# Second norm of a two-layer trunk kernel: row sums inside the output projection, scaling by rows in the lookup, first query weights loaded early

## The reference, cut to what matters

```python
for l in range(2):
    # mixing part: norm, one wide projection, four kinds of heads (4 of each)
    branches = ...                                   # retention, hgrn, gated delta, attention
    h = x + sum(gates * merged, axis=2) @ w_out      # output projection, 1024 x 1024
    y = h + peer_ffn(rms_norm(h, norm_ffn), peer_wq, peer_keys, peer_u, peer_v)

def peer_ffn(x, wq, keys, u_tab, v_tab):
    q = (x @ wq).reshape(blk, 8, 2, 128)             # 16 query tiles of 128 columns
    s = einsum('nhpd,hpkd->nhpk', q, keys)           # then two rounds of top 16, softmax g
    act = gelu(einsum('nhkd,nd->nhk', u_tab[idx], x))
    return einsum('nhk,nhkd->nd', g * act, v_tab[idx])
```

## Time and profile before

| what | value |
|---|---|
| median of 3 runs | 6624.28 us (6622.97 to 6627.76) |
| profiled execution, its own time | 6626.84 us |
| its span | 6625.2 us |
| TensorE busy | 6229.8 us, 94% of the span |
| VectorE, ScalarE busy | 54%, 32% |
| mean granted TensorE clock | 0.964 of 2.4 GHz |
| DMA | 804 MB, 121 GB/s over the span |

### The profile page before, as it was taken

How to read it: one execution, slowest core, us unless ns; L and a number is a source line. 1 busy time by engine, 2 the same in 40 slices (tenths; PEclk the granted TensorE clock), 3 DMA queues, 4 the chain that set the end, 5 groups by cost and what they waited for, 6 DMA issues and landing times. The chain is left out here.

```text
span 6625.2 us, 109110 instructions
## 1 busy us (share of the span) xinstructions
PE 6229.8 (94%) x42728; PEld 5837.3 (88%) x42728; DVE 3589.1 (54%) x6665; ACT 2142.5 (32%) x3178; POOL 0.7 (0%) x6
## 2 busy tenths in 40 slices
PE   8999988979999999999989999889799999999999
PEld 6777768979999989999967777689799999899999
DVE  3444353337788875555434443433377888755554
ACT  2333333222234442222223333232222344422222
POOL 0000000000000000000000000000000000000000
PEclk9999988989999999999999999899899999999999
DMA  3212212224346665454322122122243466654543
GB/s 103 66 50 76 65 40 74 81 89 122 113 131 181 181 196 213 168 181 167 134 94 70 50 73 70 37 75 77 92 124 112 128 188 179 194 210 170 180 167 138
DMA packets 494713, 804.32 MB, mean 121 GB/s; under 512 B 81716, under 2 KB 303156, under 8 KB 476212
## 3 DMA queue, kind: packets, MB, share of 16 engines
q1 hardware_dynamic: 494436, 800.67, 37.9%
HBM read 616.20 MB, written 186.72 MB: 121 GB/s over the span
## 5 line engine op out<-in xcount | busy, mean ns | idle before, releaser
L1652 PE MATMUL ps<-parts,wh 128*128 128x288 f32 x9216 | 1856.2, 297 | 43.7 <-DVE wl L1882 43.7
L1652 PEld LDWEIGHTS ps<-parts,wh 128*128 128x128 f32 x9216 | 1472.9, 188 | 46.9 <-DVE wl L1882 44.6
L1652 PE MATMUL ps<-parts,wl 128*128 128x288 f32 x4608 | 1356.5, 294 | 0.0
L2091 PE MATMUL ps<-parts,vh 128*128 128x320 f32 (+1 forms) x4096 | 886.5, 297 | 37.5 <-DVE gl L2163 32.1
L2091 PE MATMUL ps<-gl,vh 128*128 128x320 f32 (+1 forms) x4096 | 878.7, 295 | 0.0
L2091 PE MATMUL ps<-parts,vl 128*128 128x320 f32 (+1 forms) x4096 | 874.5, 294 | 0.0
L1652 PEld LDWEIGHTS ps<-parts,wl 128*128 128x128 f32 x4608 | 867.8, 188 | 0.0
L2168 DVE TENSOR_TENSOR vl<-third,vh 128x512 fp32r<-128x512 f32 x512 | 352.7, 689 | 675.5 <-ACT vh L2111 675.5
L2111 ACT CAST vh<-third 128x512 fp32r<-128x512 f32 x512 | 317.1, 620 | 1163.4 <-PE ps L2091 1132.2
L2091 PEld LDWEIGHTS ps<-parts,vh 128*128 128x128 f32 x4096 | 623.7, 188 | 50.0 <-issue 32.7
L2091 PEld LDWEIGHTS ps<-parts,vl 128*128 128x128 f32 x4096 | 631.4, 189 | 0.0
(11 more groups left out here) (384 smaller groups left out, 8159.1 us busy)
## 6 DMA issues: line engine op xcount, KB each, us to landing
raw<-in_u SPq DMA_DIRECT2D x256, 512.0 KB, 4.0
third<-in_v SPq DMA_DIRECT2D x512, 256.0 KB, 2.8
activated<-go SPq DMA_DIRECT2D x256, 288.0 KB, 4.3
coefficients<-wt SPq DMA_DIRECT2D x34, 2048.0 KB, 9.3
wr<-in_w_cm SPq DMA_DIRECT2D x104, 512.0 KB, 4.5
first<-activated SPq DMA_DIRECT2D x32, 1152.0 KB, 5.6
gb<-activated SPq DMA_DIRECT2D x32, 1152.0 KB, 5.6
wb<-coefficients SPq DMA_DIRECT2D x32, 1152.0 KB, 8.1
```

The costliest lines, as they stand in the source:

```text
L1652: last = nc.tensor.matmul(out, wp[:, slot, k, :], xp[:, k, cols], start=(k == 0 and wp is T.wh and xp is T.xh), stop=(k == KD - 1 and wp i ...
L2091: last = nc.tensor.matmul(out, vp[:, x % 4, m * P:(m + 1) * P], gp[:, row, col:col + size], start=begins, stop=False, skip_group_check=True)
```

## The change

1. The norm stage is gone. In the output stage ScalarE squares row k after it was added (`square`), four slots in turn, and TensorE sums it with two matmuls placed behind the product of the next tile (`total`), in PSUM banks 4 and 5, which the stage did not use. After the last sum ScalarE takes Ln and Exp into `T.rsn`.
2. In the lookup stage VectorE scales row by row (`scale`) into four slots, ScalarE copies the high part, VectorE subtracts the low part (`x_low`). The first two products are made together, row by row (`first_products`).
3. The first four query weight tiles are loaded in the output stage, behind the last of its own weights, and the first three of them are split there. The wait for the residual's write moves to the third tile of SyncE's loop in the lookup.
4. In the hgrn stage ScalarE copies the turned keys, between its takes of projections 4 and 5, instead of VectorE.
5. Buffers are placed anew so that the residual, the row scale, the squares, the ring and its split parts live across the two stages.

```diff
@@ hgrn_stage
-            for u in range(2, 6):
+            for u in range(2, 5):
                 take(u)
+            act.wait_ge(s["turned"], 1)
+            nc.scalar.copy(T.kt[:], bank(T, 6, NP_).rearrange("p (t k) -> p t k", t=TILES)
+                           ).then_inc(s["keys_ready"], 1)
+            take(5)
...
-            dve.wait_ge(s["turned"], 1)
-            nc.vector.tensor_copy(T.kt[:], bank(T, 6, NP_).rearrange("p (t k) -> p t k", t=TILES)
-                                  ).then_inc(s["keys_ready"], 1)
@@ out_stage
+            for n in range(WRING):
+                sp.dma_start(T.raw[:, n], T.d["w_query"][l, n]).then_inc(s["next_in"], 16)
             sp.wait_ge(s["added"], KD + 2)
-            sp.dma_start(T.d["xs"].rearrange("m p n -> p m n"), T.h[:]).then_inc(s["x_out"], 16)
-            sp.wait_ge(s["x_out"], 16)
+            sp.dma_start(T.d["xs"].rearrange("m p n -> p m n"), T.h).then_inc(s["x_out"], 16)
+            sp.wait_ge(s["next_in"], 16 * WRING)
...
+            def total(k):
+                pe.wait_ge(s["squared"], k + 1)
+                for a in range(2):
+                    last = nc.tensor.matmul(bank(T, 4 + a)[:, 0:HALF], T.ones, T.sq[:, k % 4, a * HALF:(a + 1) * HALF],
+                                            start=(k == 0), stop=(k == KD - 1))
+                last.then_inc(s["summed"], 1)
...
                 last.then_inc(s["produced"], 1)
+                if n:
+                    total(n - 1)
+            total(KD - 1)
...
+            def square(k):
+                act.wait_ge(s["added"], k + 3)
+                if k >= 4:
+                    act.wait_ge(s["summed"], k - 3)
+                nc.scalar.activation(T.sq[:, k % 4, :], T.h[:, k, :], ACT.Square).then_inc(s["squared"], 1)
...
             for n in range(2, KD):
                 high(n)
+                square(n - 2)
+            act.wait_ge(s["next_in"], 16 * WRING)
+            for n in range(LEAD):
+                nc.scalar.copy(T.wh[:, n], T.raw[:, n]).then_inc(s["next_high"], 1)
+            square(KD - 2)
+            square(KD - 1)
+            act.wait_ge(s["summed"], KD)
+            nc.scalar.activation(two(T.rsn), halves(T, 4), ACT.Ln, bias=T.eps, scale=1.0 / D).then_inc(s["scaled"], 1)
+            act.wait_ge(s["scaled"], 1)
+            nc.scalar.activation(T.rsn, T.rsn, ACT.Exp, scale=-0.5).then_inc(s["rooted"], 1)
+            act.wait_ge(s["rooted"], 1)
...
+                if n == KD - 2:
+                    for i in range(LEAD):
+                        dve.wait_ge(s["next_high"], i + 1)
+                        nc.vector.tensor_tensor(T.wl[:, i], T.raw[:, i], T.wh[:, i].bitcast(F32), ALU.subtract
+                                                ).then_inc(s["next_low"], 1)
@@ lookup_stage
             for n in range(WRING):
-                load_static(n)
+                sp.sem_inc(raw_in[n], 16)
             sp.dma_start(T.keys, T.d["keys"][l]).then_inc(s["keys_in"], 16)
             for n in range(TILES_STATIC):
                 sp.wait_ge(s["low"], n + LEAD + 1)
+                if n == 2:
+                    sp.wait_ge(s["x_out"], 16)
...
+            def first_products():
+                pe.wait_ge(s["low"], 2)
+                pe.wait_ge(s["drained"], 2)
+                for k in range(KD):
+                    pe.wait_ge(s["x_low"], k + 1)
+                    for n in range(2):
+                        for a in range(2):
+                            for wp, xp in ((T.wh, T.xh), (T.wh, T.xl), (T.wl, T.xh)):
+                                last = nc.tensor.matmul(bank(T, 2 * n + a)[:, 0:HALF], wp[:, n, k, :],
+                                                        xp[:, k, a * HALF:(a + 1) * HALF],
...
+            first_products()
+            scores(0)
+            for n in range(2, TILES_STATIC):
                 product(n, n % 2, n % WRING)
...
+            for k in range(KD):
+                act.wait_ge(s["normed"], k + 1)
+                nc.scalar.copy(T.xh[:, k, :], T.scaled[:, k % 4, :]).then_inc(s["x_high"], 1)
...
+            scale(0)
+            scale(1)
+            for k in range(KD):
+                x_low(k)
+                if k + 2 < KD:
+                    if k >= 2:
+                        dve.wait_ge(s["x_low"], k - 1)
+                    scale(k + 2)
             for i in range(2):
                 last = nc.vector.memset(T.qt[i], 0.0)
             last.then_inc(s["zeroed"], 1)
...
-            lows(0, LEAD + 1)
+            lows(LEAD, 1)
```

More of the change, by code:

```diff
@@ L194 @@
 W_SEMS = ("w0", "w1", "w2", "w3")
[L197 to L230, removed]
 def entry_stage(nc, T, l):
@@ L1545, in out_stage @@
 def out_stage(nc, T, l):
-    with stage(nc, "w_even", "w_odd", "x_in", "m_high", "m_low", "high", "low", "produced", "added", "x_out"
-               ) as (block, s):
+    with stage(nc, "w_even", "w_odd", "x_in", "m_high", "m_low", "high", "low", "produced", "added", "squared", "summed",
+               "scaled", "rooted", "next_in", "next_high", "next_low", shared=T.bridge) as (block, s):
         w_in = (s["w_even"], s["w_odd"])
@@ L1617, in _ @@
                     low(n + 2)
+                if n == KD - 2:
[3 more added lines that the diff above has]
+                                                ).then_inc(s["next_low"], 1)
+            dve.wait_ge(s["next_low"], LEAD)
+            dve.wait_ge(s["added"], KD + 2)
 ROWS = 8
@@ L1665, in lookup_stage @@
                "g0", "g1", "g2", "g3", "idx_ready", "eq_ready", "rows", "summed", "halved", "evicted", "w_even", "w_odd",
-               shared=T.bridge) as (block, s):
+               "normed", "x_high", "x_low", shared=T.bridge) as (block, s):
         raw_in = (s["raw0"], s["raw1"], s["raw2"], s["raw3"])
@@ L1777, in sums @@
                 last.then_inc(s["summed"], 1)
-            for n in range(TILES_STATIC):
+            def first_products():
[8 more added lines that the diff above has]
+                                                        xp[:, k, a * HALF:(a + 1) * HALF],
+                                                        start=(k == 0 and wp is T.wh and xp is T.xh),
+                                                        stop=(k == KD - 1 and wp is T.wl))
+                        if k == KD - 1:
+                            last.then_inc(s["used"], 1)
+            first_products()
+            scores(0)
+            for n in range(2, TILES_STATIC):
                 product(n, n % 2, n % WRING)
@@ L1820, in _ @@
             act.sem_inc(s["used"], WRING)
-            for n in range(LEAD):
-                high(n, n // WRING + 1, n % WRING)
+            act.sem_inc(s["high"], LEAD)
             for n in range(TILES_STATIC):
+                if n == 0:
+                    act.wait_ge(s["zeroed"], 1)
                 high(n + LEAD, (n + LEAD) // WRING + 1, (n + LEAD) % WRING)
@@ L1873, in _, with scale, x_low @@
             dve.sem_inc(s["summed"], 1)
+            dve.sem_inc(s["low"], LEAD)
+            link = chained(dve, s["chain_v"])
+            v = nc.vector
+            def scale(k):
+                nc.vector.scalar_tensor_tensor(out=T.scaled[:, k % 4, :], in0=T.h[:, k, :],
+                                               scalar=T.pl[:, L_NF + k:L_NF + k + 1], in1=T.rsn,
+                                               op0=ALU.mult, op1=ALU.mult).then_inc(s["normed"], 1)
+            def x_low(k):
+                dve.wait_ge(s["x_high"], k + 1)
+                nc.vector.tensor_tensor(T.xl[:, k, :], T.scaled[:, k % 4, :], T.xh[:, k, :].bitcast(F32),
+                                        ALU.subtract).then_inc(s["x_low"], 1)
+            scale(0)
[6 more added lines that the diff above has]
+                    scale(k + 2)
             for i in range(2):
@@ L2265, in program @@
         with nc.Fori(0, DEPTH) as l, ExitStack() as layer:
+            T.bridge = {n: layer.enter_context(nc.semaphore(n)) for n in ("early_a", "early_v", "w_first", "w_tail",
+                                                                          "g_tail", "x_out")}
+            T.pl = sb(layer, "pl", [P, PL_W])
             with ExitStack() as ctx:
                 T.xn = sb(ctx, "xn", [P, KD, NP_])
-                T.pl = sb(ctx, "pl", [P, PL_W])
-                T.br = sb(ctx, "br", [P, 16, N])
                 rs = sb(ctx, "rs", [P, N])
                 T.rs = two(rs[:])
+                before_out = ctx.enter_context(ExitStack())
+                T.br = sb(before_out, "br", [P, 16, N])
                 with ExitStack() as sub:
@@ L2318, in program @@
                 T.xh, T.xl = parts[:, 0:KD, :], parts[:, KD:2 * KD, :]
[L2319 to L2340, removed]
@@ new lines, in program @@
+                with ExitStack() as merging:
+                    wm = sb(merging, "wm", [P, 12, P])
+                    early = T.br[:, 0:3, :].rearrange("p a n -> p (a n)")[:, 0:12 * P]
+                    T.wm = (wm[:], early.rearrange("p (k c) -> p k c", k=12))
```

(27 more changed lines are left out.)

13 lines of the change are left out of this document (2 added, 11 removed).

## The result

The kernel after took 6668.89 us (median of 4 runs, 6662.04 to 6671.41), beside 6624.02 us (6622.97 to 6627.76) of the kernel before: ratio 1.0068, 95% interval 1.0053 to 1.0084. It is 45 us slower, where the prediction had it 89 us faster. Its profiled execution took 6667.4 us, its span is 6665.8. Two executions of one kernel of the experiments, `shift200`, took 8277 and 16850 us at a mean clock of 0.70 and 0.59, which nothing here explains; they are left out of its median.

What follows compares the result with a forecast made beforehand. TensorE is busy 94%, so time goes where it idles or runs slowly. Terms: 62.7 us between output projection and lookup, 7.5 key copies, 19.1 clock, together 89.3, giving 6535 us from the median; range 6520 to 6549.

Steps and rivals of the forecast that it cites:

- The step that failed: From the lookup's first query product on: an earlier start was to bring the end forward by the same amount.
- the rivals: Clock gives no help, 0.14; late weights, refill or start, 0.08; slower output projection, 0.02; residual write or loads still waiting, 0.04.
- the slower one: Output projection: float32 sums and waits bring TensorE to half clock, 48 us lost a layer, 6650 us; chance 0.02.
- end of output product to first query product: Between output projection and lookup: TensorE's distance falls from 47 to about 9 us.
- Ln to the end of Exp: ScalarE between output projection and lookup: Ln to the start of VectorE's scaling takes 2.8 us, table load included.
- the hole, both layers: TensorE's stretch between output projection and lookup: shortened to 15.4 us, gaining 31.6 and 31.1 us, together 62.7.
- copy and clock, eight heads: Hgrn stage: 7.5 us from ScalarE copying the turned keys, 19.1 us from two of three heads regaining full clock.
- all: Whole kernel: 62.7 + 7.5 + 19.1 = 89.3 us gained, 6535 us from the median of the runs.
- Early weights and refill at nothing: Output and lookup stages: early query weights and the ring's later refill cost nothing; bounds 3 and 2.3 us a layer.
- The drain of 1.38 us: ScalarE's table load between Ln and Exp: a drain would lengthen the path an estimated 1.4 us a layer.
- one of three as lost: Hgrn stage: of three half-clock heads, two taken as recovered, 19.1 us; bounds none and all three, 28.6.
- filling the gaps did not only help: Hgrn stage: by the rule that activity lifts the clock, filling TensorE's gap could only help.

Runs made afterwards that it cites:

- shift200: Kernel after with 400 satisfied TensorE waits (200 instructions) ahead of the value stage's loop; 6619.1 us (median of six runs), ratio 1.0000 to the kernel before.
- pad16: Kernel after with 16 satisfied TensorE waits (8 instructions) ahead of the value stage's loop; 6537.02 us, ratio 0.9872 to the kernel before.
- seam_pad16: `pad16` with the turned keys copied by VectorE again, as before the change; 6562.75 us, ratio 0.9904 to the kernel before.
- keys_only: Kernel before with only the turned keys' copy moved to ScalarE; 6602.22 us, ratio 0.9965 to the kernel before.
- shift4: Kernel after with 8 satisfied TensorE waits (four instructions) ahead of the value stage's loop; 6531.84 us, ratio 0.9866 to the kernel before.
- shift180: Kernel after with 360 satisfied TensorE waits (180 instructions) ahead of the value stage's loop; 6552.90 us, ratio 0.9898 to the kernel before.
- keys_late: `pad16` with ScalarE's copy of the turned keys held until VectorE's masks are done; 6550.13 us, ratio 0.9891 to the kernel before.

## Why the prediction was wrong, by its own steps

**The step that failed** stands at the end of its first part: "a start that is earlier makes the end earlier by as much". It took the value stage as carried along unchanged. The stage came 45.3 us earlier in the first layer and took 62.7 us longer than before, since the edit had moved TensorE's loop by 8 instructions, from seven blocks into eight. None of the rivals had a cause of this kind; the slower one looked for a clock fall in the output projection, which ran at full clock behind its first 6 us (5 us in the kernel before). The count of instructions was to be had from the code, and that the loop was read once from the trace of before: 9 transfers of 16.4 KB in its value stage. Which side of the edge the loop would fall on was not to be read from the trace, since the stream's offset in its blocks isn't shown; a chance for it was.

What the move cost, from the profiles: in the first layer 51.5 us of gaps, and 909.3 - 840.4 - 51.5 = 17.4 us of slower running and small waits behind them, 68.9 in all. In the second layer the loop itself takes 889.1 us for 824.1, 65.0 more, which makes 134 us in both. By the timed runs, after less `pad16`, it is 132, or 130 by their ratios.

**The other steps**, with the loop in a good place:

| step | predicted | measured |
|---|---|---|
| end of output product to first query product | about 9 us | 9.3 us |
| Ln to the end of Exp | 2.8 us | 2.74 us |
| the hole, both layers | 62.7 us | 63.9 us (`seam_pad16`) |
| copy and clock, eight heads | 26.6 us | 24.4 (`keys_only`), 25.7 (`pad16` to `seam_pad16`) |
| all | 89.3 us, 6535 | 89.6 us, 6537 (`pad16`) |

Early weights and refill at nothing: right. SyncE issues the four early loads at 1377.17, 26 us ahead of the last add, and no query product behind the first has idle time of 0.4 us or more before it. The drain of 1.38 us that the Trainium skill (ScalarE: Activation LUTs, What ACT_TABLE_LOAD costs) puts beside a table load is not in the row: Ln starts at 1406.23, Exp ends at 1408.97, and 0.74 + 1.28 + 0.68 is all but 0.04 of it.

The term for copy and clock was right in its sum by luck, since two errors offset each other. No head is at half clock now, where I took one of three as lost; by the prediction's own prices that is 28.6 + 7.5 = 36.1 us, and 24.4 and 25.7 were measured. In the profiles of `keys_only`, of `pad16` and of the kernel after, the ends of three attention stages of the first layer have 13.7 us of half clock each (the first from 305 us on), where the kernel before had 6.8. Part of what the heads gave was taken back there; filling the gaps did not only help. Why the clock fell there is not shown.

**What stays open.** Why eight blocks are fetched again at every jump and seven are not, although 2048 instructions would be eight blocks: the runs show the two cases, not what the fetching does inside. Why the gap is 7.3 us in the kernel after and two of up to 2.8 us, some 5.6 us apart, in the two kernels moved by 200. In the kernel after only the first few instructions of the loop lie in the first of the eight blocks, in the others about 50 to 60 do, so that they have work to issue while the next block comes. That would fit, and was not tested.

## What to carry to other kernels

Where TensorE runs a long hardware loop (here 1602 instructions), an edit anywhere ahead of it can move it over a block's edge. Before judging such an edit, compare the instruction queue's row and the idle time at the turns between the two pages, and time the edit with the loop moved by a few instructions. Idle time by "issue" at even distances, one less than the turns, is a sign; the count of instruction transfers is the surer one, since in the kernels moved by 200 the idle time at the jump was put down to VectorE. Here eight spare instructions turned a result of 1.0068 into 0.9872; an unlucky place would have thrown away a good change. The good window is an estimated 190 instructions wide of 256, by the theory's figures; the runs show it to be at least 176 (from `shift4` to `shift180`) and under 200 (from the kernel after to `shift200`). So the loop should be set in the middle of it. A shorter loop would have a wider window by the same working, which was not run.

## What the runs showed of the hardware that I had not expected

- A loop of 1602 TensorE instructions runs its eight turns without a further instruction transfer, or with nine at each jump (294 or 296 transfers for 168), by its place alone. The edges found are between 0 and 4, and between 180 and 200 instructions of shift, which agrees with a loop that is kept while it lies over seven blocks and not over eight. The Trainium skill (Runtime: NRT & Kernel Launch, Instruction fetch mechanics) also says "A taken branch whose target isn't in the current 2-page window forces a DMA fetch". For this loop the measurement decides: with seven blocks the jump goes back six blocks and fetches nothing: in `pad16` the value stage of the first layer shows 8 transfers for eight turns.
- In the kernel after each jump cost TensorE 7.3 us of idle time on average (6.9 to 8.0), and, behind the one looked at, 5 us at the level of 1.2 GHz. In the kernel before moved by 200 fetching again cost about half as much in all: 64 us for 132.
- A satisfied wait on TensorE took 36 ns, and 360 of them in front of a stage were not hidden.
- A gap of 0.67 us that follows one of 1.46 by 1.24 us of products was followed by 20 us of half clock in two heads of eight (`keys_late`); the first gap alone was not in any of 40.
